# A hybrid decoder block on one core: the weight splits and products of GpSimd stand in VectorE's program

## The chip, the core and the metric

One core of a Trainium2 chip runs the whole kernel. The metric is the device time in microseconds from start to end of the program, the median of several runs. The kernel before took 1029.55 us (median of 3 runs, 1029.33 to 1031.06).

The engines are named as in the profile: PE is TensorE (its matmuls; PEld its weight loads), DVE is VectorE, ACT is ScalarE, POOL is GpSimd, SP is SyncE, which here only issues DMAs. Each engine works through its own program in order, and they meet through semaphores.

## The reference, cut to what matters

One sequence of 512 tokens with 1024 features goes through one layer: two mixers side by side, then a gated MLP. All is float32.

```python
mod = c_act @ w_ada[l] + b_ada[l]                  # 6 vectors: shift, scale, gate, twice
h = modulate(rmsnorm(x, g_norm1[l]), shift1, scale1)
z = h @ w_in[l]
xr, gr, q, k, v, fl, mg = jnp.split(z, split_idx, axis=-1)
xr = causal_dwconv(xr, w_rnn_conv[l], b_rnn_conv[l])
hr = rg_lru(xr, w_lru_a[l], b_lru_a[l], w_lru_i[l], b_lru_i[l], lru_lambda[l])
y_rnn = jax.nn.gelu(gr, approximate=True) * hr
y_attn = forgetting_attention(...)
g_r, g_a = jnp.split(jax.nn.sigmoid(mg), 2, axis=-1)
merged = g_r * (y_rnn @ w_proj_rnn[l]) + g_a * (y_attn @ w_proj_attn[l])
x = x + gate1[:, None, :] * (merged @ w_out[l])
h = modulate(rmsnorm(x, g_norm2[l]), shift2, scale2)
gf, uf = jnp.split(h @ w_ffn_up[l], 2, axis=-1)
gf = causal_dwconv(gf, w_ffn_conv[l], b_ffn_conv[l])
x = x + gate2[:, None, :] * ((jax.nn.gelu(gf, approximate=True) * uf) @ w_ffn_down[l])
```

In `rg_lru`, with r and i two sigmoid gates of block-diagonal products of x: `a = exp(-8 r softplus(-lam))`, `u = sqrt(1 - a*a) * (i * x)`, and the output is the scan `h[t] = a[t] h[t-1] + u[t]`.

## The kernel before, in words

**Products in three matmuls.** Each float32 operand is split into a high part (`HI`, what the matmul's float32r format keeps) and a low part (`LO`, the rest). A product is three matmuls, LO by HI, HI by LO and HI by HI (`mm3`, lines 1425, 1426, 1427), all accumulating into one bank of PSUM (`ps`). `project` is a row of such triples over the 8 (or 10) tiles of the contraction.

**Weight chunks.** All weights come in chunks of up to 128 x 2048 values in one global order. Chunk c goes through slot c % 2 of a ring of two: SP loads it to `wraw`, ACT writes the high part (`hi`, line 569, semaphore `w_hi`), then the low part `wraw - HI` is written by `lo` (semaphore `w_lo`), and PE works on it and counts `w_used`. `w_lo` is one counter for all chunks, so the low parts are made in chunk order. PE waits for `whole(c)`, the low part of chunk c. SP loads a slot anew when the low part of its last chunk is made. Most low parts are DVE's (line 902). POOL's (line 524) are the first two chunks `C_RNN`, `C_RNN + 1`, the six gate chunks `C_MIX + 3 + 2j` of 128 x 1024, and `C_UP + 1`.

**Stages, in PE's order.**
- Head: the modulation vectors, of 512 columns each (`ada`, with index 0 to 3 here); DVE turns PE's sums into columns of `mod` (`ada_store`, lines 937, 943, 946), then makes the eight tiles of `h` (`htmp`, line 1016, then ACT's high part, then DVE's low part, line 1012). PE starts with `project2` on `C_RNN`, which takes `h` tile by tile as it is made.
- Recurrent stage (`rnn_step`, five iterations of 256 channels): PE does the xr chunk (48 matmuls), the gr chunk (48) and the block-diagonal gates (12); DVE does the convolution, the splits, and for the iteration before it the decay (`decay`), the scan (`recur`) and the split of y (`y_split`). Two kinds of products are POOL's: `ig = ig * xc` (line 534) and `gl = gl * th` (line 539), two of each per iteration.
- Mix stage: six iterations j. PE: `proj_rnn` on chunk `C_MIX + 2 + 2j` (30 matmuls, reads `yrnn`), then `gate_mr` on chunk `C_MIX + 3 + 2j` (24 matmuls, line 1425 with `h`), then `ada_total(4 + j)` (2 matmuls, lines 1457 and 1458). Before the loop PE does two more `gate_mr` and 24 matmuls for the forget gates (`fws`). DVE in iteration j: `ada(4 + j)` (eight multiply-adds, lines 911 and 914, and a split, 924 and 926), `gate_product(j)` (1139), the low part of chunk `C_MIX + 4 + 2j` (902), and `ada_store(4 + j)`, which waits for `ada_total(4 + j)`.
- Attention and the output projection, then the head of the MLP (the tiles of `h` again, lines 1329 and 1325), twelve up steps (`up_step`), the down projection, and the last norm.

These lines set the order between PE and DVE in the mix stage (PE's loop has them in this sequence):

```python
proj_rnn(C_MIX + 2, 2, j)
te.wait_ge(sigr_done, j + 2)
gate_mr(C_MIX + 3, 0, j)
ada_total(4 + j)
```

and `gate_mr` begins with `te.wait_ge(w_lo, whole(c0, i))`, `ada_store(idx)` with `ve.wait_ge(ada_mm, idx + 1)`.

Of the kernel before, what the change touches and what calls it, by code (L numbers as in the profile page):

```python
# [19 lines left out]
FP32 = mybir.dt.float32  # L20
# [3 lines left out]
ALU = mybir.AluOpType  # L24
# [3 lines left out]
P = 128  # L28
# [3 lines left out]
KD = D // P  # L32
DR = 1280
NR = DR // P
# [6 lines left out]
RING = 2  # L41
# [11 lines left out]
C_RNN = 0  # L53
C_MIX = C_RNN + NR
# [3 lines left out]
C_UP = C_OUT + KD // 2  # L58
# [22 lines left out]
def hybrid_block(nc, x, c, w_ada, b_ada, g_norm1, w_in, w_rnn_conv, b_rnn_conv, w_lru_a, b_lru_a,  # L81
# [4 lines left out]
    with ctx:  # L86
# [11 lines left out]
        HI, LO = 0, 1  # L98
        h = at("h", 0, [P, 2, KD, T], F32R)
        wsplit = at("wsplit", 32, [P, RING, 2, 2048], F32R)  # L100
# [125 lines left out]
        w_hi = sem("w_hi")  # L226
# [123 lines left out]
        def whole(c0, i=0, stride=2):  # L350

            return c0 + RING + 1 + stride * i
# [149 lines left out]
        @block.gpsimd  # L502
        def _(pool):
            pool.memset(ident[:, :], 0.0).then_inc(consts, 1)
            pool.memset(maskb[:, :], 0.0).then_inc(consts, 1)
            pool.wait_ge(consts, 2)
            pool.affine_select(out=ident[:, :], in_=ident[:, :], compare_op=ALU.not_equal, fill=1.0,
                               base=0, pattern=[[-1, P]], channel_multiplier=1).then_inc(consts, 1)

            pool.affine_select(out=maskb[:, :], in_=maskb[:, :], compare_op=ALU.is_ge, fill=MASKED,  # L510
                               base=0, pattern=[[-1, P]], channel_multiplier=1).then_inc(consts, 1)
            pool.wait_ge(consts, 4)
            pool.tensor_copy(identb[:, :], ident[:, :]).then_inc(consts, 1)
            pool.memset(ones[:, :], 1.0).then_inc(consts, 1)
            pool.memset(onesrow[:, :], 1.0).then_inc(consts, 1)
            pool.wait_ge(consts, 6)
            pool.tensor_copy(ones_r[:, :], ones[:, :]).then_inc(consts, 1)

            def lo(c0, i=0, n=2048):

                s = c0 % 2
                pool.wait_ge(w_hi, c0 + 1 + 2 * i)
                pool.wait_ge(w_lo, c0 + RING + 2 * i)
                pool.tensor_tensor(wsplit[:, s, LO, 0:n], wraw[:, s, 0:n], wsplit[:, s, HI, 0:n].bitcast(FP32),  # L524
                                   ALU.subtract).then_inc(w_lo, 1)
            lo(C_RNN)
            lo(C_RNN + 1)

            with pool.Fori(0, NR // 2) as i:
                for t in range(2):  # L530

                    pool.wait_ge(sig_done, 4 * i + t + 1)
                    pool.wait_ge(conv_tap, 6 * i + 3 * t + 3)
                    pool.tensor_tensor(ig[:, t], ig[:, t], xc[:, t], ALU.mult).then_inc(ix_done, 1)
                for t in range(2):

                    pool.wait_ge(gelu_done, 2 * i + t + 1)
                    pool.wait_ge(scan_done, 2 * i + t + 1)
                    pool.tensor_tensor(gl[:, t], gl[:, t], th[:, t], ALU.mult).then_inc(y_done, 1)

            with pool.Fori(0, KD - 2) as j:
                lo(C_MIX + 3, j, KD * P)
            lo(C_UP + 1)

            def shift(b):
                for half in range(2 if b < NB - 1 else 1):
                    cs = slice(T * half, T * half + T)  # L550
                    pool.wait_ge(o_mul, 2 * b + half + 1)
                    pool.tensor_tensor(o_nat[:, b, cs], o_nat[:, b, cs], bc[:, 1, cs], ALU.add).then_inc(o_add, 1)
            for b in range(NB - 1):
                pool.wait_ge(x2_mul, 2 * b + 2)
                pool.tensor_tensor(x2[:, b, T:D], x2[:, b, T:D], x1_nat[:, b, T:D], ALU.add).then_inc(x2_add1, 1)
                if b:
                    shift(b - 1)
            shift(NB - 2)
            shift(NB - 1)
# [336 lines left out]
        def _(ve):  # L896
            F = FP32

            def lo(c0, i=0, n=2048, stride=2):
                s = c0 % 2  # L900
                ve.wait_ge(w_hi, c0 + 1 + stride * i)
                ve.tensor_tensor(wsplit[:, s, LO, 0:n], wraw[:, s, 0:n],  # L902
                                 wsplit[:, s, HI, 0:n].bitcast(F), ALU.subtract).then_inc(w_lo, 1)
# [105 lines left out]
            def h_low(k):  # L1009

                ve.wait_ge(h_hi, k + 1)
                ve.scalar_tensor_tensor(h[:, LO, k], htmp[:, k % 2], mod[:, M_SH1 + k:M_SH1 + k + 1],  # L1012
                                        h[:, HI, k].bitcast(F), ALU.add, ALU.subtract).then_inc(h_lo, 1)
            for k in range(KD):
                wait_from(ve, h_lo, k - 1)
                ve.scalar_tensor_tensor(htmp[:, k % 2], xT_out[:, k], gs1[:, k:k + 1], ps[:, 7, :],
                                        ALU.mult, ALU.mult).then_inc(h_tmp, 1)
                if k:
                    h_low(k - 1)
            h_low(KD - 1)  # L1020

            def conv(i, t):

                ve.wait_ge(conv0, 2 * i + t + 1)
                for d in range(1, 4):
                    if d > 1:
                        ve.wait_ge(conv_tap, 6 * i + 3 * t + d - 1)
                    ve.scalar_tensor_tensor(xc[:, t, d:T], ps[:, t, 0:T - d],  # L1029
                                            vec[:, ds(V_CW + (3 - d) * NR + t + 2 * i, 1)], xc[:, t, d:T],  # L1030
                                            ALU.mult, ALU.add).then_inc(conv_tap, 1)
# [9 lines left out]
            def lru_low(i):  # L1041
                ve.wait_ge(lru_hi, 1 + i)
                ve.tensor_tensor(lru_w[:, LO].rearrange("p a n d -> p (a n d)"),
                                 lru_raw[:, :].rearrange("p a n d -> p (a n d)"),
                                 lru_w[:, HI].rearrange("p a n d -> p (a n d)").bitcast(F), ALU.subtract)\
                  .then_inc(lru_lo, 1)

            def decay(i, pair=(0, 1)):
# [9 lines left out]
                for t in pair:  # L1058
                    ve.wait_ge(a_done, 2 * i + t + 1)
                    ve.scalar_tensor_tensor(ev[:, t], av[:, t], 1.0, ev[:, t], ALU.add, ALU.mult)\  # L1060
                      .then_inc(q_done, 1)

            def recur(i, t):
                ve.wait_ge(sqrt_done, 2 * i + t + 1)
                ve.wait_ge(ix_done, 2 * i + t + 1)
                ve.tensor_tensor(ig[:, t], ev[:, t], ig[:, t], ALU.mult).then_inc(u_done, 1)  # L1066
                ve.wait_ge(u_done, 2 * i + t + 1)
                ve.tensor_tensor_scan(th[:, t], av[:, t], ig[:, t], 0.0, ALU.mult, ALU.add)\  # L1068
                  .then_inc(scan_done, 1)

            def y_split(i, t):
                ve.wait_ge(y_done, 2 * i + t + 1)
                ve.tensor_copy(yrnn[:, HI, 2 * i + t], gl[:, t]).then_inc(y_part, 1)  # L1073
                ve.wait_ge(y_part, 4 * i + 2 * t + 1)
                ve.tensor_tensor(yrnn[:, LO, 2 * i + t], gl[:, t], yrnn[:, HI, 2 * i + t].bitcast(F),  # L1075
                                 ALU.subtract).then_inc(y_part, 1)

            def rnn_step(i, inner=True):
                if inner:
                    lo(C_RNN + 1, i)  # L1080
                lru_low(i)
                conv(i, 0)
                xr_split(i, 0)
                if inner:
                    decay(i - 1)
                conv(i, 1)
                xr_split(i, 1)
                lo(C_RNN + 2, i)
                if inner:
                    recur(i - 1, 0)  # L1090
                    recur(i - 1, 1)
                    y_split(i - 1, 0)
                    y_split(i - 1, 1)

            ve.wait_ge(w_lo, RING + 2)
            rnn_step(0, inner=False)

# [27 lines left out]

            i = NR // 2 - 1
            lo(C_MIX + 1, 0, KD * P)
            decay(i, (0,))
            lo(C_MIX + 2, 0, NR * P)  # L1130
            decay(i, (1,))
# [4 lines left out]
            def gate_product(j, c0, i=0):  # L1136
                ve.wait_ge(sigr_done, j + 1)
                ve.wait_ge(w_used, whole(c0, i))
                ve.tensor_tensor(merged_a[:, j], ps[:, 2 if c0 != C_MIX + 15 else 1, :], merged_a[:, j], ALU.mult)\
                  .then_inc(mixa_done, 1)  # L1140
            with ve.Fori(0, KD - 2) as j:
                ada(4 + j)
                gate_product(j, C_MIX + 2, j)
                ve.wait_ge(w_lo, whole(C_MIX + 3, j))
                lo(C_MIX + 4, j, NR * P)
                ada_store(4 + j)
            lo(C_MIX + 15, 0, NR * P)
# [219 lines left out]
                if idx is not None:  # L1367
                    ada_store_row(idx)

            ve.wait_ge(w_lo, C_UP + RING + 2)  # L1370
            up_step(0, lambda i: lo(C_UP + 2, i), weights=False)
            ve.wait_ge(bc_loaded, 48)
            with ve.Fori(1, 7) as i:
                up_step(i, lambda i: lo(C_UP + 2, i), 9 + i)
# [447 lines left out]
```

## Time and profile before

| what | value |
|---|---|
| median of 3 runs | 1029.55 us (1029.33 to 1031.06) |
| the profiled execution, first to last instruction | span 1029.3 us, 0.25 us below the median |
| mean granted PE clock | 0.985 |
| busy: PE, PEld, DVE, ACT, POOL | 985.2, 811.6, 629.4, 401.0, 76.3 us |
| PE idle | 44.1 us, of it 17.6 in the first 60 us and 17.6 behind 1003 us |
| line 524, low parts by POOL | 9 instructions, 28.4 us |
| lines 534 and 539, products by POOL | 20 instructions, 29.6 us |

A row of the timeline has start and duration in us, then engine, line, operation and names; in brackets the idle time just before it and what ended it.
### The profile page before, as it was taken

The numbers are of one execution on the slowest core, as the hardware profiler recorded it, in microseconds if no ns is written. First come the engines' busy times: TensorE is split into PE (matmuls) and PEld (weight loads), VectorE is DVE, ScalarE is ACT, GpSimd is POOL, SyncE is SP. The second block draws the span as 40 slices with busy tenths as digits, with TensorE's granted clock in tenths as the row PEclk, the third lists the DMA queues.
The fourth block names the chain that finished last, engine by engine and source line by source line (L and its number), as shares of the span: only waits on it lengthen the run. The fifth ranks groups of instructions, "written<-read, shape, count | busy, mean of one in ns | idle before, by whom it ended". The sixth has DMA issues, their size and how long they took to land.

```text
span 1029.3 us, 12764 instructions
## 1 busy us (share of the span) xinstructions
PE 985.2 (96%) x4629; PEld 811.6 (79%) x4629; DVE 629.4 (61%) x817; ACT 401.0 (39%) x501; POOL 76.3 (7%) x51
## 2 busy tenths in 40 slices
PE   7699999899999999999999989999999999999993
PEld 3478888578889898988888878888888888888882
DVE  2788999889944537363656355677765435323238
ACT  4147786622233536262632244223222223232231
POOL 0111222411100000000000010000000000000005
PEclk9989999999999999999999999999999999999997
DMA  9813331487552323222142326656633322322302
GB/s 339 281 59 93 92 93 43 150 255 243 178 172 83 103 82 102 82 65 91 69 164 82 123 67 220 203 164 200 207 104 101 112 92 82 123 82 85 119 1 82
DMA packets 107384, 130.84 MB, mean 127 GB/s; under 512 B 4589, under 2 KB 85205, under 8 KB 106973
## 3 DMA queue, kind: packets, MB, share of 16 engines
q1 hardware_dynamic: 105392, 126.12, 37.7%
q10 hardware_dynamic: 1964, 4.35, 1.2%
q8 instruction: 18, 0.29, 0.1%
q14 instruction: 10, 0.07, 0.0%
HBM read 126.25 MB, written 4.21 MB: 127 GB/s over the span
## 4 chain that ended last, share of the span: by engine, by line
PE 77%; DVE 15%; issue 4%; DMA 2%; ACT 2%; DVEq 0%; ACTq 0%; SPq 0%
PE ps L1425 25%; PE ps L1427 24%; PE ps L1426 24%; DVE wsplit L902 3%; DMA ada_first<-in_w_ada 2%; DVE xc L1029 2%; DVE ada_acc L914 2%; PE ps L1465 1%; PE ps L1625 1%; DVE th L1068 1%; DVE ig L1066 1%; DVE o_nat L1414 1%; DVE yrnn L1073 1%; DVE yrnn L1075 1%; DVE mod L946 0%
## 5 line engine op out<-in xcount | busy, mean ns | idle before, releaser
L1425 PE MATMUL ps<-h,wsplit 128*128 128x512 f32 x864 | 340.8, 394 | 12.4 <-DVE h L1012 6.7
L1427 PE MATMUL ps<-h,wsplit 128*128 128x512 f32 x864 | 338.9, 392 | 0.0
L1426 PE MATMUL ps<-h,wsplit 128*128 128x512 f32 x864 | 338.4, 392 | 0.0
L569 ACT ACTIVATE wsplit<-wraw 128x2048 fp32r<-128x2048 f32 (+1 forms) x86 | 153.4, 1784 | 228.1 <-PE ps L1427 210.1
L902 DVE TENSOR_TENSOR wsplit<-wraw,wsplit 128x2048 fp32r<-128x2048 f32 (+1 forms) x77 | 173.1, 2248 | 108.1 <-ACT wsplit L569 107.6
L1425 PEld LDWEIGHTS ps<-h,wsplit 128*128 128x128 f32 x864 | 163.9, 190 | 46.9 <-issue 4.7
L1426 PEld LDWEIGHTS ps<-h,wsplit 128*128 128x128 f32 x864 | 163.9, 190 | 33.8
L1427 PEld LDWEIGHTS ps<-h,wsplit 128*128 128x128 f32 x864 | 163.4, 189 | 34.5
L1425 PE MATMUL ps<-wsplit,act_s 128*128 128x512 f32 x192 | 74.8, 389 | 0.2 <-DVE act_s L1342 0.2
L1426 PE MATMUL ps<-wsplit,act_s 128*128 128x512 f32 x192 | 74.7, 389 | 0.0
L1427 PE MATMUL ps<-wsplit,act_s 128*128 128x512 f32 x192 | 74.7, 389 | 0.0
L1355 DVE SCALAR_TENSOR_TENSOR cv<-ps,vec,cv 128x511 f32<-128x511 f32 (+1 forms) x48 | 35.8, 748 | 53.0 <-ACT cv L863 49.9
L914 DVE SCALAR_TENSOR_TENSOR ada_acc<-ada_raw,small,ada_acc 128x512 f32<-128x512 f32 x84 | 63.2, 752 | 3.0
L524 POOL TENSOR_TENSOR wsplit<-wraw,wsplit 128x1024 fp32r<-128x1024 f32 (+1 forms) x9 | 28.4, 3152 | 437.7 <-ACT wsplit L569 427.5
L863 ACT ACTIVATE cv<-ps,vec 128x512 f32<-128x512 f32 x24 | 18.6, 779 | 95.7 <-PE ps L1427 95.7
L1365 DVE TENSOR_TENSOR act<-gg,ps 128x512 f32 (+1 forms) x24 | 16.5, 686 | 43.2 <-PE ps L1427 43.0
L1425 PEld LDWEIGHTS ps<-wsplit,act_s 128*128 128x128 f32 x192 | 36.0, 188 | 8.2 <-issue 0.6
L1426 PEld LDWEIGHTS ps<-wsplit,act_s 128*128 128x128 f32 x192 | 36.0, 188 | 7.5
L1427 PEld LDWEIGHTS ps<-wsplit,act_s 128*128 128x128 f32 x192 | 36.0, 188 | 7.4
L1175 DVE SCALAR_TENSOR_TENSOR qk<-ps,qk 128x512 fp32r<-128x512 f32 x16 | 11.0, 690 | 47.7 <-ACT qk L725 47.7
L1426 PE MATMUL ps<-wsplit,h 128*128 128x256 f32 x128 | 36.2, 283 | 0.0
L1427 PE MATMUL ps<-wsplit,h 128*128 128x256 f32 x128 | 36.2, 283 | 0.0
(227 smaller groups left out, 1272.0 us busy)
## 6 DMA issues: line engine op xcount, KB each, us to landing
wraw<-in_w_in SPq DMA_DIRECT2D x26, 1024.0 KB, 5.2
wraw<-in_w_ffn_up SPq DMA_DIRECT2D x24, 1024.0 KB, 5.1
ada_raw<-in_w_ada SPq DMA_DIRECT2D x16, 1024.0 KB, 5.2
wraw<-in_w_ffn_down SPq DMA_DIRECT2D x12, 1024.0 KB, 4.9
ada_first<-in_w_ada SPq DMA_DIRECT2D x8, 1024.0 KB, 16.7
ada_raw<-in_w_ada_final SPq DMA_DIRECT2D x8, 1024.0 KB, 5.1
wraw<-in_w_proj_rnn SPq DMA_DIRECT2D x8, 640.0 KB, 4.3
wraw<-in_w_in SPq DMA_DIRECT2D x8, 512.0 KB, 3.9
```

Of the source, the lines that this page charges most:

```text
L524: pool.tensor_tensor(wsplit[:, s, LO, 0:n], wraw[:, s, 0:n], wsplit[:, s, HI, 0:n].bitcast(FP32), ALU.subtract).then_inc(w_lo, 1)
L569: ae.activation(wsplit[:, s, HI, 0:n], wraw[:, s, 0:n], ACT.Copy).then_inc(w_hi, 1)
L863: ae.activation(cv[:, t], ps[:, t, :], ACT.Identity, scale=vec[:, ds(V_FW + 2 * NF + t + 2 * i, 1)], bias=vec[:, ds(V_FB + t + 2 * i, 1)]) ...
L902: ve.tensor_tensor(wsplit[:, s, LO, 0:n], wraw[:, s, 0:n], wsplit[:, s, HI, 0:n].bitcast(F), ALU.subtract).then_inc(w_lo, 1)
L914: ve.scalar_tensor_tensor(acc, w, cact[:, k:k + 1], acc, ALU.mult, ALU.add)\
L1029: ve.scalar_tensor_tensor(xc[:, t, d:T], ps[:, t, 0:T - d], vec[:, ds(V_CW + (3 - d) * NR + t + 2 * i, 1)], xc[:, t, d:T], ALU.mult, ALU.a ...
L1175: ve.scalar_tensor_tensor(qk[:, t, which, LO], ps[:, t, :], SCALE if which == 0 else 1.0, qk[:, t, which, HI].bitcast(F), ALU.mult, ALU.su ...
L1355: ve.scalar_tensor_tensor(cv[:, t, d:T], ps[:, t, 0:T - d], vec[:, ds(V_FW + (2 - d) * NF + t + 2 * i, 1)], cv[:, t, d:T], ALU.mult, ALU.a ...
L1365: ve.tensor_tensor(act[:, 2 * i + t], gg[:, t], ps[:, 2 + t, :], ALU.mult)\
L1425: te.matmul(dst, lhs(LO), rhs(HI), start=start, stop=False)
L1426: te.matmul(dst, lhs(HI), rhs(LO), start=False, stop=False)
L1427: return te.matmul(dst, lhs(HI), rhs(HI), start=False, stop=stop)
```

## The change

POOL keeps its constants and its part of the last stage. Its `lo`, and its two kinds of products, go to DVE. Where they stand there: `lo(C_RNN)` ahead of the first tile of `h` and `lo(C_RNN + 1)` behind the last one; `ig * xc` (`gated_input`) behind `lru_low`, ahead of the convolution; `gl * th` at the beginning of `y_split`; `lo(C_MIX + 3, j)` behind `ada(4 + j)`, ahead of `gate_product(j)`; `lo(C_UP + 1)` behind the last tile of the second `h`. The waits on `w_lo` for POOL's parts go.

```diff
-            def lo(c0, i=0, n=2048):
-
-                s = c0 % 2
-                pool.wait_ge(w_hi, c0 + 1 + 2 * i)
-                pool.wait_ge(w_lo, c0 + RING + 2 * i)
-                pool.tensor_tensor(wsplit[:, s, LO, 0:n], wraw[:, s, 0:n], wsplit[:, s, HI, 0:n].bitcast(FP32),
-                                   ALU.subtract).then_inc(w_lo, 1)
-            lo(C_RNN)
-            lo(C_RNN + 1)
...
-                    pool.tensor_tensor(ig[:, t], ig[:, t], xc[:, t], ALU.mult).then_inc(ix_done, 1)
...
-                    pool.tensor_tensor(gl[:, t], gl[:, t], th[:, t], ALU.mult).then_inc(y_done, 1)
...
-            with pool.Fori(0, KD - 2) as j:
-                lo(C_MIX + 3, j, KD * P)
-            lo(C_UP + 1)
@@
+            lo(C_RNN)
             for k in range(KD):
                 wait_from(ve, h_lo, k - 1)
...
             h_low(KD - 1)
+            lo(C_RNN + 1)
@@
+            def gated_input(i):
+                for t in range(2):
+                    ve.wait_ge(sig_done, 4 * i + t + 1)
+                    ve.tensor_tensor(ig[:, t], ig[:, t], xc[:, t], ALU.mult).then_inc(ix_done, 1)
@@
             def y_split(i, t):
+                ve.wait_ge(gelu_done, 2 * i + t + 1)
+                ve.wait_ge(scan_done, 2 * i + t + 1)
+                ve.tensor_tensor(gl[:, t], gl[:, t], th[:, t], ALU.mult).then_inc(y_done, 1)
@@
                 lru_low(i)
+                if inner:
+                    gated_input(i - 1)
                 conv(i, 0)
@@
             lo(C_MIX + 1, 0, KD * P)
+            gated_input(i)
             decay(i, (0,))
@@
             with ve.Fori(0, KD - 2) as j:
                 ada(4 + j)
+                lo(C_MIX + 3, j, KD * P)
                 gate_product(j, C_MIX + 2, j)
-                ve.wait_ge(w_lo, whole(C_MIX + 3, j))
                 lo(C_MIX + 4, j, NR * P)
                 ada_store(4 + j)
@@
-            ve.wait_ge(w_lo, C_UP + RING + 2)
-            up_step(0, lambda i: lo(C_UP + 2, i), weights=False)
+            up_step(0, lambda i: lo(C_UP + 2, i))
```

DVE's mix loop before, from the last multiply-add of `ada` on (`wsplit` of 128x1280 is the low part of chunk `C_MIX + 4 + 2j`, `ada_diag` is the beginning of `ada_store`):

```order
L924 CAST ada_split<-ada_acc 128x512
...
L926 TENSOR_TENSOR ada_split<-ada_acc,ada_split 128x512
...
L1139 TENSOR_TENSOR merged_a<-ps,merged_a 128x512
...
L902 TENSOR_TENSOR wsplit<-wraw,wsplit 128x1280
...
L937 TENSOR_TENSOR ada_diag<-ps,ident 128x512
```

The same place in the changed kernel (line 897 is the cast that was 924):

```order
L897 CAST ada_split<-ada_acc 128x512
...
L899 TENSOR_TENSOR ada_split<-ada_acc,ada_split 128x512
...
L875 TENSOR_TENSOR wsplit<-wraw,wsplit 128x1024
...
L1124 TENSOR_TENSOR merged_a<-ps,merged_a 128x512
...
L875 TENSOR_TENSOR wsplit<-wraw,wsplit 128x1280
...
L910 TENSOR_TENSOR ada_diag<-ps,ident 128x512
```

The low part of the gate chunk (128x1024) now stands behind the whole of `ada(4 + j)` on DVE, and so also behind the `ada_store(3 + j)` of the iteration before; before, it was in POOL's program, behind nothing but its own semaphores.

DVE's end of the recurrent stage in the changed kernel (`gl` is the new product, `ig` of 1041 the other):

```order
L875 TENSOR_TENSOR wsplit<-wraw,wsplit 128x1024
L1041 TENSOR_TENSOR ig<-ig,xc 128x512 x2
L1027 SCALAR_TENSOR_TENSOR ev<-av,th 128x512
...
L1048 SCALAR_TENSOR_TENSOR th<-av,ig 128x512
L1054 TENSOR_TENSOR gl<-gl,th 128x512
L1056 CAST yrnn<-gl 128x512
L1058 TENSOR_TENSOR yrnn<-gl,yrnn 128x512
```

Four DVE instructions of 128x512 stand there that were POOL's.

## Rows read from the trace of the kernel before

**Rows 1.** The page, busy time of each engine.
```profile
PE 985.2 (96%) x4629; PEld 811.6 (79%) x4629; DVE 629.4 (61%) x817; ACT 401.0 (39%) x501; POOL 76.3 (7%) x51
```

**Rows 2.** Timeline of the head: start us, us, engine, line, names [idle before].
```profile
42.80 4.52 POOL L524 TENSOR_TENSOR wsplit<-wraw,wsplit 128x2048 fp32r<-128x2048 f32 x1 [39.74 <-ACT wsplit L569]
42.84 4.50 DVE L946 TENSOR_TENSOR mod<-mod,vec 128x4 f32<-128x4 f32 x1
...
47.26 0.21 DVE L999 TENSOR_TENSOR fws<-fw,fws 128x64 fp32r<-128x64 f32 x1
...
49.23 1.41 DVE L1016 SCALAR_TENSOR_TENSOR htmp<-xT_out,small,ps 128x512 f32<-128x512 f32 x2
...
51.66 0.47 PE L1425 MATMUL ps<-h,wsplit 128*128 128x512 f32 x1 [4.54 <-DVE h L1012]
...
53.84 4.52 DVE L1012 SCALAR_TENSOR_TENSOR h<-htmp,mod,h 128x512 fp32r<-128x512 f32 x1
...
58.41 0.50 PE L1425 MATMUL ps<-h,wsplit 128*128 128x512 f32 x1 [2.17 <-DVE h L1012]
...
63.39 1.63 DVE L1012 SCALAR_TENSOR_TENSOR h<-htmp,mod,h 128x512 fp32r<-128x512 f32 x2
```

**Rows 3.** Windows: length, then PE, PEld, DVE, ACT, POOL, clock, DMA.
```profile
68.30:79.18 10.88, 10.88 (x50) 9.01 (x48) 10.03 (x19) 4.07 (x4) 0.00 (x0) 1.00 0.10 26
...
179.82:185.30 5.48, 5.48 (x25) 4.32 (x23) 5.19 (x6) 2.37 (x3) 3.13 (x3) 1.00 0.38 112
...
189.14:196.10 6.96, 6.96 (x24) 5.56 (x25) 4.25 (x7) 6.83 (x8) 0.00 (x0) 0.79 0.85 273
...
213.90:228.27 14.37, 13.10 (x57) 10.54 (x57) 12.94 (x17) 2.82 (x3) 2.39 (x1) 1.00 0.95 293
228.27:240.96 12.69, 12.69 (x57) 10.51 (x56) 11.45 (x15) 2.82 (x3) 2.39 (x1) 1.00 0.72 204
...
266.94:280.17 13.23, 12.97 (x57) 10.43 (x56) 12.64 (x16) 2.82 (x3) 2.39 (x1) 1.00 0.52 167
```

**Rows 4.** Timeline of DVE in the recurrent loop, one iteration.
```profile
111.15 3.37 DVE L902 TENSOR_TENSOR wsplit<-wraw,wsplit 128x2048 fp32r<-128x2048 f32 x1
...
125.39 2.29 DVE L902 TENSOR_TENSOR wsplit<-wraw,wsplit 128x2048 fp32r<-128x2048 f32 x1
...
132.82 1.55 DVE L1075 TENSOR_TENSOR yrnn<-gl,yrnn 128x512 f32 x1
...
136.40 3.38 DVE L902 TENSOR_TENSOR wsplit<-wraw,wsplit 128x2048 fp32r<-128x2048 f32 x1
```

**Rows 5.** Timeline at the end of the recurrent stage, ACT, PE and DVE.
```profile
182.92 1.28 ACT L644 ACT_TABLE_LOAD   x1 [4.50 <-DVE th L1068]
...
189.14 0.79 PE L1425 MATMUL ps<-h,wsplit 128*128 128x512 f32 x1 [3.72 <-DVE wsplit L902]
...
191.71 0.69 DVE L1052 SCALAR_TENSOR_TENSOR ev<-av,th 128x512 f32<-128x512 f32 x1 [2.63 <-ACT th L663]
...
203.41 2.61 DVE L1073 CAST yrnn<-gl 128x512 fp32r<-128x512 f32 x1
...
206.67 0.48 DVE L911 TENSOR_SCALAR ada_acc<-ada_raw,small 128x512 f32<-128x512 f32 x1
```

**Rows 6.** Timeline of DVE, one iteration of the mix stage.
```profile
228.92 0.69 DVE L937 TENSOR_TENSOR ada_diag<-ps,ident 128x512 f32<-128x512 f32 x1 [1.49 <-PE ps L1458]
...
230.57 2.12 DVE L946 TENSOR_TENSOR mod<-mod,vec  x1
...
239.71 0.69 DVE L1139 TENSOR_TENSOR merged_a<-ps,merged_a 128x512 f32 x1
240.31 1.48 DVE L902 TENSOR_TENSOR wsplit<-wraw,wsplit 128x1280 fp32r<-128x1280 f32 x1
```

**Rows 7.** Timeline at the head of the MLP.
```profile
612.31 2.47 DVE L1325 SCALAR_TENSOR_TENSOR h<-htmp,mod,h 128x512 fp32r<-128x512 f32 x1
...
614.93 0.47 PE L1425 MATMUL ps<-h,wsplit 128*128 128x512 f32 x1 [1.97 <-DVE h L1325]
```

More of the change, by code:

```diff
@@ L517, in _ @@
             pool.tensor_copy(ones_r[:, :], ones[:, :]).then_inc(consts, 1)
-            def lo(c0, i=0, n=2048):
-                s = c0 % 2
-                pool.wait_ge(w_hi, c0 + 1 + 2 * i)
-                pool.wait_ge(w_lo, c0 + RING + 2 * i)
-                pool.tensor_tensor(wsplit[:, s, LO, 0:n], wraw[:, s, 0:n], wsplit[:, s, HI, 0:n].bitcast(FP32),
-                                   ALU.subtract).then_inc(w_lo, 1)
-            lo(C_RNN)
-            lo(C_RNN + 1)
[L529 to L533, printed above, removed]
-                    pool.tensor_tensor(ig[:, t], ig[:, t], xc[:, t], ALU.mult).then_inc(ix_done, 1)
-                for t in range(2):
-                    pool.wait_ge(gelu_done, 2 * i + t + 1)
-                    pool.wait_ge(scan_done, 2 * i + t + 1)
-                    pool.tensor_tensor(gl[:, t], gl[:, t], th[:, t], ALU.mult).then_inc(y_done, 1)
-            with pool.Fori(0, KD - 2) as j:
-                lo(C_MIX + 3, j, KD * P)
-            lo(C_UP + 1)
             def shift(b):
@@ L1093, in rnn_step @@
                     y_split(i - 1, 1)
-            ve.wait_ge(w_lo, RING + 2)
             rnn_step(0, inner=False)
```

## The prediction

> **What bounds the kernel now.** The page first: PE is busy for 985.2 of 1029.3 us and DVE for 629.4 [rows 1]. PE's work does not change, so the change can move the time only where PE waits, or where it runs at half clock after a wait. I therefore went through the waits of PE, then through the windows of the stages for PE's busy time and its clock, and then through the timeline around each wait.
>
> In the undisturbed stretches PE sets the pace: 48 matmuls in 10.88 us at clock 1.00 [rows 3], that is 0.2267 us each.
>
> The head shows what POOL's work costs DVE. POOL's low part runs from 42.80 for 4.52 us, and DVE's add on 128x4 values, begun at 42.84, takes 4.50 us; the tile at 53.84 takes 4.52 us in the same way [rows 2], where the two at 63.39 take 1.63 together. DVE stands still until POOL is done. PE waits for both: 4.54 us ahead of its first matmul on `h`, and 2.17 us at 58.41 [rows 2].
>
> In the recurrent loop PE has 108 matmuls an iteration, 108 x 0.2267 = 24.5 us. DVE's iteration is 136.40 - 111.15 = 25.25 us [rows 4]. DVE falls behind, and PE pays at the end, with 3.72 us at 189.14 [rows 5]. Behind it, 24 matmuls take 6.96 us at mean clock 0.79 [rows 3] in place of 24 x 0.2267 = 5.44: a wait of that size costs another 1.52 us, since PE starts again and then falls from 2.4 to 1.2 GHz for a while.
>
> In the mix stage PE's iteration is 56 matmuls, 12.7 us, and the windows from one `ada_total` to the next are 14.37, 12.69, (13.26, 12.72,) 13.23 us [rows 3]; all five from 213.90 to 280.17 make 66.27, mean 13.25. DVE is busy for 11.5 to 12.9 us in each. This is the one stage in which both engines are nearly full and depend on each other in a circle.
>
> **The change part by part.**
>
> *Head.* The add at 42.84 takes some 0.2 us again (the one at 47.26, on 128x64, takes 0.21), so DVE's next instruction starts at 43.04 in place of 47.26 [rows 2]: 4.22 us gained. `lo(C_RNN)` stands ahead of the tiles and takes 2.29 us, as an undisturbed one does [rows 4], 2.2 from start to start. The tiles start 2.0 us earlier, and PE's first matmul on them at 49.65. From there the old kernel needs 68.30 - 51.66 = 16.64 us for 48 matmuls, 5.76 more than 10.88: the wait of 2.17 and two stretches at half clock. The wait goes with POOL's second part, so one of the stretches should too; with one of them (1.5 us, as above) PE needs 12.5 us and is at `C_RNN + 1` at 62.15. Its low part: the last tile ended at 65.02 and now ends 2.0 + 3.77 us earlier, at 59.25 (3.77 is 4.52 less an undisturbed 0.75), and 2.29 us more give 61.55, just in time. **-6.1 us.** SP loads the next chunk into that slot 3.8 us later than before (61.6 in place of 57.8), more than 10 us ahead of ACT's need for it behind PE's 48 matmuls: no cost.
>
> *Recurrent loop.* Of DVE's 25.25 us go the four delays by POOL: the low part at 111.15 takes 3.37 where 2.29 is undisturbed, the subtraction at 132.82 takes 1.55 [rows 4] where 0.69 is [rows 6]; that is 1.08 and 0.86, and four of about 0.97 make 3.9 us. Four products come in; from start to start a tensor_tensor takes 0.60 us [rows 6], with a wait for its own predecessor up to 0.85, so 2.4 to 3.4 us. DVE then needs 23.8 to 24.75 us against PE's 24.5. I take 24.2: PE never waits in this loop, neither before nor after, and the loop costs **0**. The upper end would make DVE late by 0.25 us an iteration, 1 us in all.
>
> *End of the recurrent stage.* I count from G, the start of the first gate chunk on PE, 179.82 [rows 3]; it moves by -6.1 with the head. Before, `ada_total(4)` started at G + 34.1 (213.90). After, DVE is not behind, `lo(C_MIX + 1)` is made in time, and the wait of 3.72 us goes. But now the first `gate_mr` of the loop waits. ACT starts its sigmoids about G + 0.2 (before, it had to wait until 182.92 for DVE's scan), and DVE's decay follows 191.71 - 182.92 = 8.8 us behind [rows 5], at G + 9.0. From the decay to `ada(4)` DVE took 206.67 - 191.71 = 14.96 us. Two products of POOL and one low part fell into it: the cast at 203.41 took 2.61 us in place of some 0.48 (what the one-input instruction at 206.67 takes [rows 5]), and two others about 0.97 more each, 4.1 us together. These go and two products of 0.7 us come: 12.3 us, so `ada(4)` starts at G + 21.3. `ada` takes 7.1 us: it starts as the add at 230.57 ends, at 232.65, and `gate_product` follows it at 239.71 [rows 6]. Then the gate chunk's low part: no undisturbed row of 128x1024 exists; it lies between half of 2.29, 1.15, and the 1.48 of the 128x1280 one [rows 6]; on the line between 1280 and 2048 it is 1.21, and with the step to PE 1.27. PE can start `gate_mr(0)` at G + 21.3 + 7.1 + 1.3 = G + 29.6. It is ready for it at G + 23.2 (two gate chunks 10.9, the forget gates 5.5, `proj_rnn` 6.8). The wait is 6.4 us, the clock falls behind it, and with 6.96 us for the 24 matmuls `ada_total(4)` is at G + 36.6. **+2.5 us.**
>
> *Mix loop.* After, a circle closes in every iteration. `ada_total` starts on PE; DVE's `ada_store` follows 0.65 us later (two matmuls, then the step seen at 228.92); from there to the end of the next `ada` it is 239.71 - 228.92 = 10.79 less POOL's 1.9 (the add at 230.57 took 2.12, undisturbed 0.2) = 8.9 us [rows 6]; the low part and the step to PE take 1.27. So the next `gate_mr` starts 10.8 us behind `ada_total`. PE's `proj_rnn` and `ada_total` need only 7.25 of them: PE waits for 3.6 us in each iteration, as long as at 189.14, so I expect the half clock each time, and the 24 matmuls take 6.96. The period is 10.8 + 6.96 = 17.8 us in place of 13.25: +4.57, five times **+22.9 us**. DVE idles for some 4 us in each, waiting for `ada_total`. The DMAs: SP's load of the next gate chunk waits for this low part, and the two loads of `ada_raw` stand behind it in SP's queue. They move 2.5 MB in the 9.5 us until `ada` needs the first half of it; the stretch from 213.90 moved 293 GB/s [rows 3], 2.8 MB in that time: covered, but the thinnest cover of the change.
>
> *Head of the MLP.* The tile at 612.31 took 2.47 us beside POOL and PE waited for it until 614.93 [rows 7]; undisturbed it takes 0.75. PE starts 1.7 us earlier. With only 0.25 us of wait left the fall of the clock (1.5 us) may go too, but then PE meets the low part of `C_UP + 1`, 2.29 us behind the last tile. I take **-2.2 us**, between 1.7 and 2.6.
>
> The sum: -6.1 + 0 + 2.5 + 22.9 - 2.2 = +17.1 us on the profiled 1029.3, or 1046.4; the median of the runs shown is 0.25 above that execution, so **1046.6 us**.
>
> **A rule against this reading.** The Trainium skill, SBUF — State Buffer, section "Who interferes with whom", says that GpSimd has only the port pair that it shares with VectorE, and that one instruction locks out the other for its whole length. The 4.50 us beside 4.52 agree with it. By that rule alone, taking work from POOL costs DVE nothing, 2.29 us in place of 4.52, and the kernel becomes faster. It tells what an instruction costs, not where in the order it stands; the first rival is what it would give.
>
> **Rivals.**
> *Faster: PE stays covered in the mix stage.* DVE is relieved everywhere, the waits go and none come: the head -6.1, the 3.72 and 1.52 us at 189.14, the mix loop at PE's 12.7 us (5 x 0.55 = 2.8), the MLP -2.2: -16.3, 1013 us. For it: DVE's own busy time falls in each of these places. Against it: the low part must end within 7.25 us of `ada_total` and comes at 10.8; it decides for this case only if DVE does `ada_store` and `ada` 3.6 us faster, or ahead of `ada_total`, which its own wait forbids.
>
> *Same waits, full clock.* If 3.6 us of waiting after 13 us of dense work do not bring the clock down, each of six `gate_mr` takes 5.44 us: -9.1, 1037.5 us. For it: the 1.27 us gap inside the window from 213.90 left the clock at 1.00 [rows 3]. Against it: both 2.17 and 3.72 us brought it down. The Trainium skill, TensorE: Matmul & The Clock Gate, section on HAM oscillation, describes a kernel that falls back to half rate at every wait between tiles; that speaks for the forecast.
>
> *DVE becomes the bound of the recurrent loop, or the loads come late.* At 24.75 us, or with the first half of `ada_raw` late by 0.5 us in each iteration: 1 to 4 us more, 1048 to 1050 us.
>
> **Chances and range.** The forecast 0.64, full clock 0.12, a second bound 0.12, faster 0.08, something between that leaves the time as it is 0.04. The range from 1036 to 1051 leaves out the last two. 0.2% (2 us) is about what a measurement of this kernel tells from no change: faster 0.08, same 0.03, slower 0.89.
>
> **What would show it.** Head: no instruction of DVE over 3 us, PE's first matmul on `h` near 49.7. Recurrent loop: PE without a wait, DVE's period at 24.5. Mix: six waits of PE for the 128x1024 low part, the first near 6 us and five near 3.6, the clock below 0.9 in each iteration, a period of 17.8. MLP: PE's wait near 0.3 us. I am wrong if the mix period stays under 14 us, or if DVE is late in the recurrent loop by more than 1 us at its end.

## The result, and the profile after

The changed kernel takes 1054.58 us (median of 4 runs, 1053.94 to 1055.51) where the kernel before takes 1029.44 (4 runs, 1029.25 to 1031.06): 1.0238 times as long, 95% interval 1.0224 to 1.0253, some 25 us slower. The prediction's sign and mechanism held; its size did not. It gave 1046.6 us with a range up to 1051.0, and the time is 3.6 us above that range.

First the page: span, busy time of each engine, and PE's granted clock in 40 slices.

```profile
span 1053.2 us, 12688 instructions
...
PE 995.0 (94%) x4629; PEld 817.1 (78%) x4629; DVE 617.7 (59%) x846; ACT 401.3 (38%) x501; POOL 18.4 (2%) x22
...
PEclk9899999888889999999999999999999999999997
```

Against [rows 1], POOL has lost 57.9 us of work and DVE, which took that work over, is busy for 11.7 us less, not more. PE has the same 4629 matmuls and is busy for 9.8 us longer: they run at a lower clock (0.972 over the whole span, 0.985 before). The other 14.1 of the 23.9 us between the spans is time in which PE stands still. The five slices in a row with an 8 reach from 7 x 26.3 to 12 x 26.3 us, 184 to 316, which is the mix stage.

PE's waits: line waited for, us in total, times, longest. First two rows of the kernel before, then the changed kernel.

```profile
PE ps L1425 <- DVE h L1012: 6.7, 2, 4.5
PE ps L1425 <- DVE wsplit L902: 5.5, 4, 3.7
```

```profile
PE ps L1409 <- DVE wsplit L875: 25.3, 7, 6.3
PE ps L1449 <- DMA ada_first<-in_w_ada: 11.0, 2, 6.8
PE ps L1409 <- DVE h L985: 2.4, 1, 2.4
```

Before, PE waited for DVE's low parts 4 times, 5.5 us in all, and 6.7 us for the tiles `h` of the head. Now it is 7 times and 25.3 us for the low parts: 24.7 us at the six gate chunks of the loop, and 0.6 us at 181.13, at the gate chunk `C_MIX + 1` ahead of it. The waits for `h` fell as foreseen, those for `wsplit` are the new ones.

The head, timeline of DVE and PE. It answers to [rows 2].

```profile
35.04 6.73 PE L1449 MATMUL ps<-ada_first,cact_rows 128*128 128x512 f32 x8 [4.19 <-DMA ada_first<-in_w_ada]
...
44.12 0.16 DVE L919 TENSOR_TENSOR mod<-mod,vec 128x4 f32<-128x4 f32 x1
...
46.16 2.29 DVE L875 TENSOR_TENSOR wsplit<-wraw,wsplit 128x2048 fp32r<-128x2048 f32 x1
...
50.80 0.47 PE L1409 MATMUL ps<-h,wsplit 128*128 128x512 f32 x1 [2.40 <-DVE h L985]
```

The add on 128x4 values takes 0.16 us, where beside POOL it took 4.50, and the low part 2.29, where POOL needed 4.52. The Trainium skill, SBUF — State Buffer, "Who interferes with whom", says that GpSimd has only the port pair that it shares with VectorE, and that the one that comes second is blocked for the other's whole instruction. The add, long beside POOL and short without it, agrees.

The end of the recurrent stage, timelines of ACT, PE and DVE. It answers to [rows 5].

```profile
176.02 1.28 ACT L617 ACT_TABLE_LOAD   x1 [2.50 <-DVE th L1048]
...
184.82 0.69 DVE L1027 SCALAR_TENSOR_TENSOR ev<-av,th 128x512 f32<-128x512 f32 x1 [2.54 <-ACT th L636]
...
197.07 0.48 DVE L884 TENSOR_SCALAR ada_acc<-ada_raw,small 128x512 f32<-128x512 f32 x1
...
204.17 1.22 DVE L875 TENSOR_TENSOR wsplit<-wraw,wsplit 128x1024 fp32r<-128x1024 f32 x1
...
205.54 0.76 PE L1409 MATMUL ps<-h,wsplit 128*128 128x512 f32 x1 [6.32 <-DVE wsplit L875]
```

With G = 174.92, the start of the first gate chunk on PE, DVE's decay is at G + 9.9, `ada(4)` at G + 22.15 and the first `gate_mr` of the loop at G + 30.6, behind a wait of 6.32 us.

One iteration of the mix loop on DVE. It answers to [rows 6].

```profile
213.12 0.69 DVE L910 TENSOR_TENSOR ada_diag<-ps,ident 128x512 f32<-128x512 f32 x1 [5.73 <-PE ps L1442]
...
214.77 0.16 DVE L919 TENSOR_TENSOR mod<-mod,vec  x1
215.19 0.49 DVE L884 TENSOR_SCALAR ada_acc<-ada_raw,small 128x512 f32<-128x512 f32 x1 [0.26 <-issue]
215.71 5.48 DVE L887 SCALAR_TENSOR_TENSOR ada_acc<-ada_raw,small,ada_acc 128x512 f32<-128x512 f32 x7
...
222.29 1.22 DVE L875 TENSOR_TENSOR wsplit<-wraw,wsplit 128x1024 fp32r<-128x1024 f32 x1
```

DVE waits for PE's `ada_total` (L1442) for 5.73 us, then does `ada_store`, the whole of `ada` and the low part in one go, 10.4 us, and PE waits for that low part. Both engines idle in every round, each waiting for the other. No DVE row in it ends a wait for a DMA: the loads of `ada_raw` were in time.

The windows: the recurrent loop from G - 100.65 to G, and then PE's six `gate_mr`, each from the first matmul behind its wait to `ada_total`. Columns as in [rows 3].

```profile
74.27:174.92 100.65, 100.65 (x445) 83.36 (x444) 90.52 (x135) 77.48 (x88) 0.00 (x0) 1.00 0.27 84
205.54:212.47 6.93, 6.93 (x25) 5.60 (x25) 1.85 (x2) 0.00 (x0) 0.00 (x0) 0.79 0.88 296
223.57:231.62 8.05, 8.05 (x24) 6.42 (x25) 1.94 (x2) 0.00 (x0) 0.00 (x0) 0.67 0.89 304
242.71:249.83 7.12, 7.12 (x24) 5.74 (x25) 1.94 (x2) 0.00 (x0) 0.00 (x0) 0.77 0.86 289
260.92:269.09 8.17, 8.17 (x25) 6.52 (x25) 1.95 (x2) 0.00 (x0) 0.00 (x0) 0.66 0.89 304
280.18:287.31 7.13, 7.13 (x24) 5.77 (x25) 1.94 (x2) 0.00 (x0) 0.00 (x0) 0.76 0.87 291
298.39:306.59 8.20, 8.20 (x24) 6.53 (x25) 1.95 (x2) 0.00 (x0) 0.00 (x0) 0.66 0.68 208
```

The ends of these windows are the six starts of `ada_total`: 94.12 us for five periods, mean 18.82, where it was 66.27 and 13.25. A period is 11.10 us from `ada_total` to the next `gate_mr` and then 7.1 to 8.2 us for 24 matmuls that take 5.44 at full clock. The clock falls in each, to a mean of 0.66 to 0.79, between the two levels of 2.4 and 1.2 GHz.

Head of the MLP: first matmul on `h`, against 614.93 with 1.97 us of wait in [rows 7].

```profile
639.58 0.47 PE L1409 MATMUL ps<-h,wsplit 128*128 128x512 f32 x1 [0.25 <-DVE h L1310]
```

### The profile page after: what moved, and what is told of

The parts are those of the page before. It is cut to its first block, busy times and chain, and to the rows that moved or that the text cites. A ratio compares the mean times of both kernels' runs of the same rounds, so it can differ in the third digit from the quotient of the medians.

```text
span 1053.2 us, 12688 instructions
## 1 busy us (share of the span) xinstructions
PE 995.0 (94%) x4629; PEld 817.1 (78%) x4629; DVE 617.7 (59%) x846; ACT 401.3 (38%) x501; POOL 18.4 (2%) x22
## 4 chain that ended last, share of the span: by engine, by line
PE 75%; DVE 16%; issue 4%; DMA 2%; ACT 2%; DVEq 0%; ACTq 0%; SPq 0%
PE ps L1409 24%; PE ps L1411 24%; PE ps L1410 24%; DVE ada_acc L887 3%; DVE wsplit L875 2%; DMA ada_first<-in_w_ada 2%; DVE xc L1004 2%; PE ps L1449 1%; PE ps L1609 1%; DVE ig L1046 1%; DVE o_nat L1398 1%; DVE gl L1054 1%; DVE htmp L1314 0%; DVE mod L916 0%; DVE h L1310 0%
## 5 line engine op out<-in xcount | busy, mean ns | idle before, releaser
L1409 PE MATMUL ps<-h,wsplit 128*128 128x512 f32 x864 | 345.6, 400 | 28.0 <-DVE wsplit L875 25.3
L1410 PE MATMUL ps<-h,wsplit 128*128 128x512 f32 x864 | 341.4, 395 | 0.0
L1411 PE MATMUL ps<-h,wsplit 128*128 128x512 f32 x864 | 341.4, 395 | 0.0
L875 DVE TENSOR_TENSOR wsplit<-wraw,wsplit 128x2048 fp32r<-128x2048 f32 (+1 forms) x86 | 182.9, 2127 | 108.1 <-ACT wsplit L542 107.6
L1409 PEld LDWEIGHTS ps<-h,wsplit 128*128 128x128 f32 x864 | 165.8, 192 | 66.8 <-DVE wsplit L875 22.0
L1411 PEld LDWEIGHTS ps<-h,wsplit 128*128 128x128 f32 x864 | 165.3, 191 | 35.4
L1410 PEld LDWEIGHTS ps<-h,wsplit 128*128 128x128 f32 x864 | 166.0, 192 | 33.7
L1411 PE MATMUL ps<-wsplit,h 128*128 128x256 f32 x128 | 36.2, 283 | 0.0
L1410 PE MATMUL ps<-wsplit,h 128*128 128x256 f32 x128 | 36.2, 283 | 0.0
L1409 PE MATMUL ps<-wsplit,h 128*128 128x256 f32 x128 | 36.2, 283 | 0.0
```

Of the source, the lines that this page charges most:

```text
L875: ve.tensor_tensor(wsplit[:, s, LO, 0:n], wraw[:, s, 0:n], wsplit[:, s, HI, 0:n].bitcast(F), ALU.subtract).then_inc(w_lo, 1)
L1409: te.matmul(dst, lhs(LO), rhs(HI), start=start, stop=False)
L1410: te.matmul(dst, lhs(HI), rhs(LO), start=False, stop=False)
L1411: return te.matmul(dst, lhs(HI), rhs(HI), start=False, stop=stop)
```

## The experiments

The kernel before ran beside them again: 1030.36 us (7 runs) beside the first group, 1030.23 (17 runs) by the last. The ratios below are against it.

### 1. The gate chunk's low part ahead of `ada`

In the changed kernel two lines of DVE's mix loop change places:

```
-                ada(4 + j)
                 lo(C_MIX + 3, j, KD * P)
+                ada(4 + j)
```

> The changed kernel with one statement moved: the low part of the gate chunk stands ahead of ada(4 + j) on DVE, not behind it. Theory of the place (the price is the order, DVE's 1.2 us of work itself is affordable): after ada_store DVE makes the low part at once, PE finds it made, and no gate_mr of the loop waits; ada_total follows ada with about 1 us of wait in the first iteration alone; period 12.7 us in place of 18.8, the first ada_total 3.5 us earlier against its head than before the change. Sum against before: head -4.9, up to the first ada_total -3.5, loop -2.7, MLP -2.7, about 1015.6 us, ratio 0.987. Rival (DVE is simply too full in this stage, wherever the low part stands): period stays at 16 us or more, ratio 1.01 to 1.02.

Measured: 1019.02 us (1018.40 to 1020.32), ratio 0.9892 [0.9875, 0.9908], clock 0.990. PE's starts of `ada_total` and its waits in the mix loop, then DVE in its second iteration:

```profile
203.27 0.50 PE L1441 MATMUL ps<-ada_split,ones_r 128*128 128x512 f32 x1 [0.79 <-DVE ada_split L899]
...
205.27 0.75 PE L1409 MATMUL ps<-yrnn,wsplit 128*128 128x512 f32 x1 [1.26 <-DVE wsplit L875]
...
219.25 0.39 PE L1441 MATMUL ps<-ada_split,ones_r 128*128 128x512 f32 x1
...
231.94 0.39 PE L1441 MATMUL ps<-ada_split,ones_r 128*128 128x512 f32 x1
...
270.17 0.39 PE L1441 MATMUL ps<-ada_split,ones_r 128*128 128x512 f32 x1
```

```profile
207.19 1.23 DVE L875 TENSOR_TENSOR wsplit<-wraw,wsplit 128x1024 fp32r<-128x1024 f32 x1 [0.25 <-issue]
208.33 0.48 DVE L884 TENSOR_SCALAR ada_acc<-ada_raw,small 128x512 f32<-128x512 f32 x1
...
219.91 0.69 DVE L910 TENSOR_TENSOR ada_diag<-ps,ident 128x512 f32<-128x512 f32 x1 [2.39 <-PE ps L1442]
```

The same instructions on the same engines, 35.6 us faster than the changed kernel. From the second period on PE does not wait, and (270.17 - 219.25) / 4 = 12.73 us is its own 56 matmuls. What costs is the low part's place in DVE's program, behind `ada`, and not DVE's load. But DVE has little over: its wait of 2.39 us stands in the first period, which is the long one, and in the four others it waits 0.32 to 0.38 us for `ada_total`. The first period (15.98 us) still holds a wait of 1.26 us and half-rate matmuls behind it, which is about the 3.4 us by which the run misses its expectation.

### 2. The gate chunk's low part left on POOL, all other moves made

```
...
+            with pool.Fori(0, KD - 2) as j:
+                lo(C_MIX + 3, j, KD * P)
...
                 ada(4 + j)
-                lo(C_MIX + 3, j, KD * P)
                 gate_product(j, C_MIX + 2, j)
+                ve.wait_ge(w_lo, whole(C_MIX + 3, j))
```

> The changed kernel with the six low parts of the gate chunks on POOL again, and everything else on DVE. Theory: the whole loss sits in these six instructions. Mix loop at about 13.2 us a period again, one of POOL's parts delays DVE by 2 us ahead of the first; against before: head -4.9, up to the first ada_total -2.6, loop 0, MLP -2.7, about 1019 us, ratio 0.990. Rival (the products in the recurrent stage or the splits in the heads cost too): ratio 1.00 or more.

Measured: 1021.84 us (1020.99 to 1021.97), ratio 0.9916 [0.9899, 0.9932]. `ada_total` starts at 204.59 and, five periods later, at 271.04. Without the one move the change gains 8.5 us; the mix loop is where it loses.

### 3 and 5. PE kept busy during the wait

In the changed kernel dummy matmuls on 128x128 stand ahead of each `gate_mr(C_MIX + 3, ...)`, the rest is as it is. They take the half clock away and leave the circle. Experiment 3 has calls of 54 and 30, experiment 5 these:

```
+            keep_clock(24, 4)
             gate_mr(C_MIX + 3, 0)
...
+                keep_clock(14, 4)
                 gate_mr(C_MIX + 3, 0, j)
```

> The changed kernel with dummy matmuls of 128x128 into an unused bank ahead of each gate_mr of the mix loop: 54 ahead of the first, 30 ahead of the others, so that PE is busy for most of each wait (about 6.0 and 3.4 us). They add no result. Theory of the half clock: PE stays at 2.4 GHz, each of six gate_mr takes 5.45 us in place of 6.9 to 8.2 (mean 7.6), and since the circle runs through gate_mr the gain comes out whole: -12.9 us against the changed kernel, about 1041.7 us, ratio to before 1.012. Rival (the clock is off the circle, DVE's chain alone sets the period): 1054 us as the changed kernel.

Measured: 1060.88 us (1059.90 to 1061.50), ratio 1.0292 [1.0275, 1.0309], clock 0.990. It met neither expectation, and for a reason of its own, one iteration on PE:

```profile
241.12 6.86 PE L1457 MATMUL ps<-ident,ones 128*128 128x128 f32 x60
...
253.27 0.39 PE L1441 MATMUL ps<-ada_split,ones_r 128*128 128x512 f32 x1
```

A call of 30 is 60 matmuls and takes 6.86 us, more than the 3.8 us that there were to fill; the period is 7.25 + 6.86 + 5.3 = 19.4 us. The clock question stayed open, hence experiment 5, sized by this row.

> The keep_clock experiment with doses that fit the waits. A call of 30 issued 60 matmuls of 0.113 us, 6.8 us against a wait of 3.85; now 24 ahead of the first gate_mr (5.4 us against 6.3) and 14 ahead of the others (3.2 us against 3.85). Theory of the half clock: gate_mr takes 5.45 us each time, -12.9 us against the changed kernel, about 1041.7 us, ratio to before 1.012, period 16.6 us. Rival (the clock is off the circle): 1054.6 us, ratio 1.024.

Measured: 1041.04 us (1040.58 to 1044.60), ratio 1.0117 [1.0098, 1.0135], clock 0.991. One iteration on PE:

```profile
216.21 3.29 PE L1457 MATMUL ps<-ident,ones 128*128 128x128 f32 x28
...
220.05 0.50 PE L1409 MATMUL ps<-h,wsplit 128*128 128x512 f32 x1 [0.56 <-DVE wsplit L875]
...
225.66 0.39 PE L1441 MATMUL ps<-ada_split,ones_r 128*128 128x512 f32 x1
```

The low part comes when it came before: from `ada_total` at 208.95 to `gate_mr` at 220.05 it is 11.10 us, as in the changed kernel. The 24 matmuls behind it now take 5.61 us. Over the six `gate_mr` it is 33.5 us in place of 45.6 (the sum of the six windows above): **the half clock costs 12.1 us**, and the period without it is 16.7, which is the circle alone. The spans differ by 14.3 us; the other 2.2 had come before the first of the six, 2.1 of them in the head, which differs between executions (below) and which the dummy matmuls do not touch.

### 4, 6, 7, 8. Each part of the change alone

All four start from the kernel before. In 4 only the gate chunk's low part goes from POOL to DVE, behind `ada`; in 6 only `lo(C_RNN)` and `lo(C_RNN + 1)`; in 7 only the 20 products of the recurrent stage; in 8 only `lo(C_UP + 1)`. The edit of 4:

```
-            with pool.Fori(0, KD - 2) as j:
-                lo(C_MIX + 3, j, KD * P)
...
                 ada(4 + j)
+                lo(C_MIX + 3, j, KD * P)
                 gate_product(j, C_MIX + 2, j)
-                ve.wait_ge(w_lo, whole(C_MIX + 3, j))
```

> The kernel before with only the six low parts of the gate chunks moved to DVE, at the place where the change puts them. Theory: the same circle as in the changed kernel, period 18.8 us (+27.8 over five periods), and the first ada_total about 6 us later because DVE comes out of the recurrent stage late as before; none of the gains: about 1063 us, ratio 1.033. Rival (the circle closes only together with the other moves): ratio under 1.01.

> The kernel before with only the low parts of the first two chunks moved to DVE, as in the change. Theory: DVE loses 2.2 us ahead of the tiles of h and gains 4.2, and PE's wait of 2.2 us in the tiles goes with one stretch at half clock: -4.9 to -6.1 us at the start of chunk C_RNN + 1, and nothing downstream takes it back, since DVE's lag in the recurrent stage moves with the head; ratio 0.995. Rival (the gain of the head is eaten by the lag of DVE, which came late to the loop anyway): ratio 1.000.

> The kernel before with only the twenty products moved to DVE. Theory: DVE's period in the recurrent loop falls from 25.25 to 24.9 us, PE's wait of 3.72 us at its end to 0.6, and the stretch at half clock behind it goes: -4 to -4.6 us, ratio 0.996. Rival (POOL's delays and the products cost DVE the same, so nothing changes): ratio 1.000.

> The kernel before with only the low part of chunk C_UP + 1 moved to DVE. Theory: the second tile of h is not held up, PE starts 1.8 us earlier and keeps its clock: -2.7 us at the start of that chunk's matmuls, ratio 0.9974. Rival (what is gained at the tiles is lost behind the last one, where the low part now stands in DVE's way): ratio 1.000.

| only this moved | us, median (range) | ratio, 95% | difference |
|---|---|---|---|
| 4: mix low part | 1063.23 (1062.89 to 1063.87) | 1.0318 [1.0300, 1.0335] | +32.9 |
| 6: two low parts of the head | 1023.74 (1022.94 to 1026.56) | 0.9946 [0.9931, 0.9961] | -6.5 |
| 7: 20 products | 1026.24 (1025.88 to 1027.90) | 0.9966 [0.9953, 0.9979] | -4.0 |
| 8: low part of the MLP | 1028.74 (1027.76 to 1030.15) | 0.9984 [0.9975, 0.9993] | -1.5 |

Experiment 4 has the whole loss and more. Its waits in two iterations of the mix loop:

```profile
229.40 0.79 PE L1423 MATMUL ps<-h,wsplit 128*128 128x512 f32 x1 [3.82 <-DVE wsplit L900]
...
237.43 0.39 PE L1455 MATMUL ps<-ada_split,ones_r 128*128 128x512 f32 x1
...
248.63 0.79 PE L1423 MATMUL ps<-h,wsplit 128*128 128x512 f32 x1 [3.79 <-DVE wsplit L900]
...
255.64 0.39 PE L1455 MATMUL ps<-ada_split,ones_r 128*128 128x512 f32 x1
```

Its five periods take 312.45 - 218.17 = 94.28 us, as in the changed kernel (94.12). So the rest of the change neither helps nor harms that loop. The other three parts each gain. Alone their sum is -12.0 us; together they give -8.5 on top of the kernel before (experiment 2) and 1054.58 - 1063.23 = -8.7 on top of experiment 4. The traces locate the gap in part. The five periods of the mix loop take 64.8 us in experiment 6 and 66.5 in experiment 2 (66.3 before). And from the last `ada_total` to the end the kernel before needs 749.1 us, experiments 6, 7 and 8 need 748.3, 748.0 and 746.6, which is 4.4 us gained in sum, while experiment 2 gains 1.0. A piece of that is at the head of the MLP in experiment 2, on PE:

```profile
599.20 3.04 PE L1465 MATMUL ps<-ident,ones 128*128 128x128 f32 x16
```

These 16 dummy matmuls take 1.95 us at full clock, as in the changed kernel (634.11) and in experiment 1; here most ran at half, and experiment 2 needs 748.2 us from its last `ada_total` to its end where experiment 1 needs 746.6. The 0.8 us of experiment 6 is of the same kind: at the head of the MLP PE waits for `h` 1.98 us, as before (1.97), but the next 10.07 us have a clock of 1.00 where they had 0.83, and nothing there was edited. So differences of about 1 us between single traces can come from such stretches alone.

Experiment 7 did what was expected of its stage: DVE's period in the recurrent loop is 24.94 us, PE's wait at its end 0.62, and the half clock behind it is gone. But between G and the first `ada_total` it gains only 2.6 us, with two new waits for DVE in it, 0.79 and 0.68; the rest of its -4.0 lies where the edit changes nothing. Experiment 8 measured -1.5 by medians and, from the last `ada_total` to the end of its trace, -2.5, against the 2.7 expected; the trace of the kernel before is one of its slower executions (see the next section).

## Why the prediction was right about the sign and wrong about the size

By its own steps, in the profiled spans (1053.2 - 1029.3 = 23.9 us):

| step | predicted | measured | from |
|---|---|---|---|
| head, up to `xrs` | -6.1 | -4.9 | 79.18 to 74.27 |
| recurrent loop | 0 | 0.0 | 100.65 us, 100.64 before |
| G to the first `ada_total` | +2.5 | +3.5 | G + 37.55, G + 34.08 before |
| mix loop | +22.9 | +27.9 | 94.12 us, 66.27 before |
| MLP and rest | -2.2 | -2.5 | +26.4 at the last `ada_total`, +23.9 at the end |

**Right:** where the time goes and why. Six waits for the low parts of the gate chunks, the first 6.32 us (6.4 predicted) and five of 3.7 (3.6 predicted), the circle `ada_total`, `ada_store`, `ada`, low part, `gate_mr`, `ada_total`, and DVE idle inside it; experiments 1 and 4 show that this one place is the whole loss, experiments 2, 6, 7 and 8 that the rest gains. The step from `ada_total` to `gate_mr` was put at 10.8 us (10.86 in the period of 17.82 that was summed) and took 11.10, mostly a pause of 0.26 us ahead of `ada` that the sum had not counted: 1.2 us over five periods. The 12.3 us from the decay to `ada(4)` took 12.25, `ada` 7.10, the low part of 128x1024 1.22.

**The step that failed** is "the 24 matmuls take 6.96". That was one row, the window behind the one wait of 3.72 us in the old kernel. The first of the six took 6.93, but the last five took 8.05, 7.12, 8.17, 7.13 and 8.20, mean 7.73: 0.77 more, five times, **3.9 of the 5.0 us** by which the mix loop was underestimated. The mechanism, a fall of the clock at each wait, held; experiment 5 measures it at 12.1 us over six where the prediction had 6 x 1.52 = 9.1. With the 3.9 us added the forecast would have been 1050.5, inside its own range.

**G to the first `ada_total`:** 1.0 us more, and here a second step failed, "DVE is not behind". DVE's period in the recurrent loop had been put at 24.2 us, or 24.75 at most, against 24.5 of PE. PE's iteration is 24.48 us, before and after. DVE's is 24.93. One iteration of the changed kernel, timelines of DVE and ACT:

```profile
105.06 2.29 DVE L875 TENSOR_TENSOR wsplit<-wraw,wsplit 128x2048 fp32r<-128x2048 f32 x1
...
107.86 1.29 DVE L1041 TENSOR_TENSOR ig<-ig,xc 128x512 f32<-128x512 f32 x2
108.81 0.78 ACT L601 ACTIVATE xc<-ps,vec 128x512 f32<-128x512 f32 x1 [0.36 <-DVE ig L1041]
109.73 2.54 DVE L1004 SCALAR_TENSOR_TENSOR xc<-ps,vec,xc 128x511 f32<-128x511 f32 x3 [0.58 <-ACT xc L601]
...
129.99 2.29 DVE L875 TENSOR_TENSOR wsplit<-wraw,wsplit 128x2048 fp32r<-128x2048 f32 x1
```

Without the 0.58 us the period would be 24.35, less than PE's. That wait is a second, small circle that the sum did not have. ACT may write the next `xc` only when the moved product has read the last one (`conv_first` waits for `ix_done`), and DVE's convolution, right behind the product, waits for that `xc`. The kernel before has no such wait in its iterations from 105 to 165 us; there POOL made the product. So DVE falls behind by 0.45 us an iteration. PE does not wait in the loop (its cost of 0 was right) but pays behind it: the low part of `C_MIX + 1` is 0.61 us late, and ACT waits for DVE's scan until G + 1.1, where the prediction let it start at G + 0.2; all that follows stood 0.9 us later. This is the rival "DVE becomes the bound of the recurrent loop" at its small end. Whether another place of the product takes the wait away was not tried.

**Head:** 1.2 us less than predicted. PE's first matmul on `h` was expected at 49.65 and came at 50.80. The eight matmuls on `ada_first` ahead of it took 6.73 us in this execution. In five others with the same head, experiments 1, 2, 3, 5 and 6, that first matmul came at 49.24, 49.48, 49.26, 49.36 and 49.69, and in experiment 1 the eight took 5.21. So the forecast of that start was right within 0.4 us for them, and up to `xrs` they gain 6.6 to 7.1 us, more than the 6.1 predicted. How many of these eight run at half clock differs between executions; why was not tried.

**From the trace to the median:** the steps above make 6.8 of the 8.0 us by which 1046.6 was too low. The rest is the last step of the sum, which added 0.25 us to go from the profiled span before to the median. For the changed kernel that is 1054.58 - 1053.2 = 1.4 us. In every execution for which both are recorded, the time lies 1.7 to 2.3 us above the span. So the span of 1029.3 can only be that of the slowest of the three runs shown, 1031.06 us, and the sum began some 1.5 us above the median and was measured against it. Where the extra time of that execution sits in its trace is not known.

**The rivals.** "Faster" needed the low part within 7.25 us of `ada_total`; it came at 11.10. The prediction said that only a DVE faster by 3.6 us, or an order that DVE's own wait forbids, could bring that; it overlooked the order of experiment 1, where the low part goes ahead of `ada`, which depends on nothing in it. "Same waits, full clock" was worked out as 1037.5 us; made real in experiment 5 it is 1041.04. Of the 3.5 us between them 1.9 are the step from span to median; in spans it is 1038.9 against 1037.3, with periods of 16.68 us in place of 16.3. The late loads did not occur. The range was too narrow on top for a plain reason: its upper end allowed for a rival of 1 to 4 us and gave the half clock, 9.1 us of the sum, no spread of its own.

## What to carry to other kernels

What a moved instruction costs is not its duration but its place: on an engine that works in order, put work that another engine waits for ahead of long work that nobody waits for yet, and look for a circle between the engines before moving anything. This change closed two: one of PE and DVE, which cost 28 us, and one of DVE and ACT, which cost about 1. Here one swap of two lines, at equal work, is the difference between 2.4% slower and 1.1% faster, and experiment 1 (1019.02 us) is the fastest version found. A cost that repeats in a loop should get its range from more than one row; if the trace has only one, the range has to say so.

## What was not expected of the hardware

- After waits of equal length the half-rate stretch had two lengths in turn: 3.67 us of wait both at 280.18 and at 298.39, and then 7.13 and 8.20 us for the same 24 matmuls. The rhythm was the same in experiment 4 (`gate_mr` to `ada_total` 8.03, then 7.01 us). What sets which of the two comes was not found. The Trainium skill, TensorE: Matmul & The Clock Gate, section on HAM oscillation, describes a matmul kernel that falls to half rate at each of its waits between tiles. The trace agrees: behind each of the six waits the clock has a mean of 0.66 to 0.79.
- Whether the clock falls behind a shorter wait is not set by the length of the wait alone. A wait of 1.26 us ahead of the second `proj_rnn` was followed by 6.93 us at clock 1.00 in experiment 2 (1.27 us of wait, the same, in the kernel before) and by 8.54 us at 0.80 for the same matmuls in experiment 1. What else sets it was not tried.
- 28 dummy matmuls on 128x128, 3.29 us of them, in a wait of 3.85 us kept the clock: 5.6 us for the matmuls behind, though 0.56 us of wait remained. In this loop they are worth 12.1 us to the changed kernel as it stands (the medians differ by 13.5), and in experiment 1 the wait that they fill is not there.
- DVE's busy time fell by 11.7 us when it was given 29 instructions more, since POOL's two-operand instructions had held it: 4.50 us for an add of 0.16, and 2.12 for 0.16 in one of the mix iterations.
